# Gather-fed expert layer: the rest of the query projection in eighths of a block per slot, more early gather buffers, second tile's routing from slot 95

## The chip, the cores and the metric

One NeuronCore of a Trainium2 chip runs the whole program. Its engines run side by side, each through its own list of instructions, and meet at semaphores: PE (matrix products), DVE (vector operations), ACT (activations, copies), POOL (here small vector work and the indirect DMAs) and SP (plain DMAs). The metric is the device time of one execution in microseconds.

## What is computed

A transformer block of 512 tokens with 1024 channels and an expert layer, then a second block. The change is within the expert layer:

```python
def peer_ffn(h, wq, keys, u_tab, v_tab):
    ...
        q = (xb @ wq).reshape(T, PEER_HEADS, 2, PEER_KHALF)
        s = jnp.einsum('thpc,hpnc->thpn', q, keys)
        v1, i1 = lax.top_k(s[:, :, 0], PEER_TOPK)
        v2, i2 = lax.top_k(s[:, :, 1], PEER_TOPK)
        ...
        idx = jnp.take_along_axis(cidx, pos, axis=-1)
        gate = jax.nn.softmax(sc, axis=-1)
        ug = jnp.take(u_tab, idx, axis=0)
        act = jax.nn.gelu(jnp.einsum('td,thkd->thk', xb, ug), approximate=False)
        vg = jnp.take(v_tab, idx, axis=0)
        return jnp.einsum('thk,thkd->td', gate * act, vg)
```

Each token picks 8 x 16 = 128 of 16384 experts. Its 128 rows of u and v (8 KB for a pair) are gathered from HBM.

## The kernel before

`experts` (from L1935) works on four token tiles of 128 tokens. A *slot* is one of the 128 picks of every token in the tile: POOL issues an indirect DMA that brings 128 rows of u and v, 1.05 MB, into a buffer (L2115 for tile 0, L2132 behind it); DVE takes the dot of each u row with its token (`dot_slot` L2636); ACT makes gelu, the weight and a diagonal matrix of it (`gelu_slot` L2370, three instructions, the last L2378); PE multiplies the diagonal by the v rows into an accumulator (`sum_slot` L2213, instruction L2218, four matmuls of fp32). Only then is the buffer free (`used`), for which POOL waits before it issues the gather that goes there. All engines go through the slots in order; the order of all else is written out by slot numbers.

Ahead of this stand the query projection (16 blocks of 128 columns: `products`, 24 fp32r matmuls over 8 input chunks in three parts, L2155 to L2157; ACT casts the high part of the weights, `high` L2334, DVE subtracts the low part, `low` L2529, and takes the block out of PSUM, `evacuate` L2534), the scores against the keys for tile 0 (`first_score` L2161, `take_first` L2338), the normed activations h2 (`make_h2` L2537 on DVE), their turning into token rows (`turn_h` L2169 on PE, `take_h` L2342 on ACT), and routing (`route` L2544 on DVE): per group of heads eight pieces of top-k and softmax work. Two blocks belong to a head.

Tile 0 starts while the projection is unfinished. Blocks 0 to 5 (`JOINED_FROM = 6`) come first. Block 6 to 15 go into slots 0 to 39 (`CHUNKS = 4`): PE does a quarter of a block (six matmuls), then the sum of the slot `LAG = 2` behind. As the late gather buffers share memory with the projection's weights, slots 0 to 39 go round `EARLY = 4` buffers (`uv_spare`, `uv_second`, the second half of `cands`, the second half of h2, the last of which waits until h2 is turned). From slot 40, when all products are done, there are eight. Routing of tile 0: head 0 ahead of all, then head 1 from slot 0, pairs of heads from slots 12, 28, 44, one piece after each dot (`FIRST_AT`). Tile 1: two halves of four heads, one piece after every fourth dot from slot 56; its scores stand on PE behind the sum of slot 52, their copies on ACT behind slot 54. Tiles 1 to 3 run with eight buffers; tile 2's routing is spread over tile 1. Between tile 0's last sum and tile 1's first stand on PE a closing reset product, `score(2)` and an opening one, and on ACT `store(0)` and `take_scores(2)`. In tiles 2 and 3 the FFN's first half is woven in, by slot too.

Of the kernel before, what the change touches and what calls it, by code (L numbers as in the profile page):

```python
# [18 lines left out]
ALU = mybir.AluOpType  # L19
# [7 lines left out]
KD = D // P  # L27
# [1639 lines left out]
def mixer_out(nc, o, x, lnw, lnb, consts, saved_in, gate, bonus, sel, first):  # L1667


    with ExitStack() as ctx:  # L1670
# [139 lines left out]
        def _(dve):  # L1810
# [77 lines left out]
HEAD_GROUPS = (slice(0, 1), slice(1, 2), slice(2, 4), slice(4, 6), slice(6, 8))  # L1888
# [46 lines left out]
def experts(nc, w, x, weight, keys, consts, uv_tab, norm_after, ffn_in, ffn_out, ffn_weight, next_w, kept):  # L1935
# [13 lines left out]
    with ExitStack() as ctx:  # L1949
# [34 lines left out]
        with ExitStack() as first:  # L1984
# [8 lines left out]
        uv = [uv_late[:, 0], uv_late[:, 1], uv_late[:, 3], uv_late[:, 4], uv_spare[:, :, :], uv_late[:, 5], uv_late[:, 6], h2_rows]  # L1993
        uv_early = [uv_spare[:, :, :], uv_second[:, :, :], uv_third, h2_rows]
# [23 lines left out]
        squared, squared_p, added, summed, rooted, scaled, h2_made, h_turned, h_taken = map(signal, (  # L2018
            "wq_squared", "wq_squared_p", "wq_added", "wq_norm_summed", "wq_rooted", "wq_scaled", "h2_made", "h_turned", "h_taken"))
# [30 lines left out]
        def rows_of(t, at):  # L2050

            return uv_early[at % EARLY] if t == 0 and at < JOINED else uv[at % GROUPS]

# [85 lines left out]
        def _(pe):  # L2139
# [111 lines left out]

            for n in range(JOINED_FROM):
                products(n)
# [7 lines left out]
                if n == JOINED_FROM - 1:  # L2261
                    for k in range(KD // 2):
                        turn_h(k)
            for c in range(JOINED):
                n, q = JOINED_FROM + c // CHUNKS, c % CHUNKS
                products(n, q * KD // CHUNKS, (q + 1) * KD // CHUNKS)
# [1269 lines left out]
```

## Time and profile before

| | us |
|---|---|
| median of 3 runs | 2935.97 (2935.08 to 2940.54) |
| the profiled execution, its own time | 2942.34 |
| its span in the profile | 2940.5 |
| PE busy | 2652.8 (90%) |
| DVE busy | 1882.7 (64%) |
| ACT busy | 1231.4 (42%) |
| POOL busy | 755.6 (26%) |

Times in the rows are from the span's start. In an instruction's row the first number is its start, the second its length, in brackets stands how long the engine sat idle before it and who released it; several like instructions in a row are merged (x4). A window's row has for PE, weight loads, DVE, ACT and POOL the busy time and number of instructions, then PE's granted clock (1.00 is full speed), the mean share of time in which the 16 DMA engines are busy, and GB/s. A busy share of the whole span says little here: the expert layer's four tiles are one stretch of some 1400 us, and in each part of it another resource ends last.

### The profile page before, as it was taken

To read this page: it belongs to the slowest core of one execution; us is meant where nothing else is said; L and a number is where in the kernel's file an instruction comes from. 1 tells how busy PE (TensorE), PEld (TensorE's weight loads), DVE (VectorE), ACT (ScalarE), POOL (GpSimd) and SP (SyncE) were. 2 spreads that over 40 slices of the span, in tenths; PEclk is the share of its full clock that TensorE was granted. 3 is DMA by queue.
4 is the path that set the end of the run, shared out by engine and by line. 5 is a ranking of instruction groups with operands and counts; after the bars stand their busy time and mean duration, and the time that the engine had idled before them with its cause. 6 is when DMAs were issued, how large, how long until landed. Compare 5 with 4: busy or idle time off the path is not lost. (4 is left out here: it accounts for less than half of the span.)

```text
span 2940.5 us, 43930 instructions
## 1 busy us (share of the span) xinstructions
PE 2652.8 (90%) x16052; PEld 1806.7 (61%) x16052; DVE 1882.7 (64%) x3737; ACT 1231.4 (42%) x2723; POOL 755.6 (26%) x684
## 2 busy tenths in 40 slices
PE   8979999977787788899999999999899998999998
PEld 6669866533333333355555555799766676788876
DVE  6966667878867757976666665576666635554422
ACT  5622234434434444555555544443345355322221
POOL 0223212344454444444344344000100001100000
PEclk9989999999999999999999999999999999999998
DMA  4220127999999999999999999656411212223231
GB/s 158 68 70 22 43 91 287 330 382 422 421 412 415 421 414 421 414 408 419 419 419 419 420 419 419 240 185 179 139 58 58 65 51 72 89 95 96 80 132 49
DMA packets 128590, 714.84 MB, mean 243 GB/s; under 512 B 14232, under 2 KB 17176, under 8 KB 61720
## 3 DMA queue, kind: packets, MB, share of 16 engines
q0 software_dynamic: 73728, 536.90, 44.6%
q1 hardware_dynamic: 53528, 173.37, 17.6%
q8 instruction: 119, 1.95, 0.3%
q10 hardware_dynamic: 1152, 2.10, 0.2%
q14 instruction: 63, 0.52, 0.0%
HBM read 707.07 MB, written 7.86 MB: 243 GB/s over the span
## 5 line engine op out<-in xcount | busy, mean ns | idle before, releaser
L2218 PE MATMUL expert_total<-uv_rows,h 128*128 128x512 f32 x1032 | 492.5, 614 | 90.4 <-ACT h L2378 89.8
L2132 POOL DMA_INDIRECT uv_rows<-in_peer_uv,expert_ids x288 | 344.0, 1194 | 411.2 <-PE expert_total L2218 237.8
L2639 DVE CUSTOM_DVE_ANT_0 uv_rows<-uv_rows,h_tok 128x1024 f32<-128x1024 f32 x258 | 312.4, 1224 | 171.7 <-DMA uv_rows<-in_peer_uv,expert_ids 169.4
L2218 PEld LDWEIGHTS expert_total<-uv_rows,h 128*128 128x128 f32 x1032 | 188.5, 194 | 353.5 <-ACT h L2378 184.7
L2374 ACT ACTIVATE expert_acts<-expert_dots 128x1 f32<-128x1 f32 x384 | 77.6, 202 | 508.6 <-DVE expert_dots L2639 508.0
L2195 PE MATMUL expert_total<-uv_rows,h 128*128 128x512 f32 x384 | 186.9, 634 | 41.9 <-ACT h L2368 41.9
L2658 DVE TENSOR_TENSOR ffn_half_w_lo<-uv_rows,ffn_half_w_hi 128x1024 fp32r<-128x1024 f32 (+1 forms) x136 | 162.3, 1194 | 82.3 <-ACT ffn_half_w_hi L2398 78.9
L2398 ACT CAST ffn_half_w_hi<-uv_rows 128x1024 fp32r<-128x1024 f32 (+1 forms) x136 | 137.8, 1014 | 113.6 <-PE score_out L2249 63.3
L2195 PEld LDWEIGHTS expert_total<-uv_rows,h 128*128 128x128 f32 x384 | 75.2, 203 | 150.8 <-issue 120.3
L2247 PE MATMUL score_out<-ffn_half_x_hi,ffn_half_w_hi 128*128 128x256 f32 x528 | 167.8, 318 | 0.0
L2631 DVE CUSTOM_DVE_ANT_0 uv_rows<-uv_rows,h_tok 128x1024 f32<-128x1024 f32 x96 | 116.3, 1225 | 69.0 <-DMA uv_rows<-in_peer_uv,expert_ids 68.3
L2378 ACT ACTIVATE h<-const_sb,expert_weights 128x128 f32<-128x128 f32 x384 | 154.3, 402 | 12.5
L2249 PE MATMUL score_out<-ffn_half_x_hi,ffn_half_w_lo 128*128 128x256 f32 x528 | 149.8, 284 | 0.0
L2248 PE MATMUL score_out<-ffn_half_x_lo,ffn_half_w_hi 128*128 128x256 f32 x528 | 149.7, 284 | 0.0
L299 PE MATMUL ffn_in_out<-ffn_h_hi,ffn_in_w_hi 128*128 128x512 f32 x350 | 141.0, 403 | 2.5 <-DVE ffn_in_w_lo L388 2.5
L301 PE MATMUL ffn_in_out<-ffn_h_hi,ffn_in_w_lo 128*128 128x512 f32 x350 | 140.0, 400 | 0.0
L300 PE MATMUL ffn_in_out<-ffn_h_lo,ffn_in_w_hi 128*128 128x512 f32 x350 | 140.0, 400 | 0.0
L2978 PE MATMUL mix_out<-h_hi,mix_w_hi 128*128 128x512 f32 x303 | 128.5, 424 | 3.1 <-DVE mix_w_lo L3252 3.1
L379 DVE TENSOR_TENSOR ffn_in_w_lo<-ffn_in_w,ffn_in_w_hi 128x1024 fp32r<-128x1024 f32 x43 | 52.7, 1225 | 108.2 <-ACT ffn_in_w_hi L329 108.2
L2980 PE MATMUL mix_out<-h_hi,mix_w_lo 128*128 128x512 f32 x303 | 120.2, 397 | 0.0
L2979 PE MATMUL mix_out<-h_lo,mix_w_hi 128*128 128x512 f32 x303 | 120.0, 396 | 0.0
L2218 PE MATMUL expert_total<-h 128*128 128x512 f32 x212 | 104.3, 616 | 16.2 <-ACT h L2378 16.2
(578 smaller groups left out, 6447.6 us busy)
## 6 DMA issues: line engine op xcount, KB each, us to landing
uv_rows<-in_ffn_w_in SPq DMA_DIRECT2D x88, 512.0 KB, 6.1
ffn_in_w<-in_ffn_w_in SPq DMA_DIRECT2D x43, 512.0 KB, 3.5
mix_w<-in_w_in SPq DMA_DIRECT2D x39, 512.0 KB, 3.5
uv_rows<-in_ffn_w_out SPq DMA_DIRECT2D x32, 512.0 KB, 4.2
last_w<-in_ffn_w_out SPq DMA_DIRECT2D x7, 1408.0 KB, 6.2
w_in<-in_w_in SPq DMA_DIRECT2D x19, 512.0 KB, 3.5
wq_w<-in_peer_wq SPq DMA_DIRECT2D x15, 512.0 KB, 4.0
uv_rows<-in_ffn_w_out SPq DMA_DIRECT2D x16, 384.0 KB, 3.7
```

Of the source, the lines that this page charges most:

```text
L299: nc.tensor.matmul(out[:, b], high, hi[:, k], start=(k == 0), stop=False)
L300: nc.tensor.matmul(out[:, b], high, lo[:, k], start=False, stop=False)
L301: mm = nc.tensor.matmul(out[:, b], low, hi[:, k], start=False, stop=(k == kt - 1))
L2132: nc.gpsimd.indirect_dma_start(out=uv[first + j].rearrange("p a d -> p (a d)"), out_offset=None, in_=uv_tab, in_offset=bass.IndirectOffset ...
L2195: mm = nc.tensor.matmul(total[:, t % 2, half], diag[:, b], v[b][:, half * T:(half + 1) * T], start=False, stop=False)
L2218: mm = nc.tensor.matmul(total[:, t % 2, half], diag[:, b], rows_of(t, at)[:, 1, half * T:(half + 1) * T], start=False, stop=False)
L2247: nc.tensor.matmul(ffn_bank(n), high, x_high, start=(k == 0), stop=False)
L2248: nc.tensor.matmul(ffn_bank(n), high, x_low, start=False, stop=False)
L2249: mm = nc.tensor.matmul(ffn_bank(n), low, x_high, start=False, stop=(k == blocks - 1))
L2378: nc.scalar.activation(diag[:, b], consts("ident"), ACT.Copy, scale=scale_[:, col]).then_inc(diagonals, 1)
L2639: a.tensor_tensor_reduce(out=rows, in0=rows, in1=h_tok[:, t], scale=1.0, scalar=0.0, op0=ALU.mult, op1=ALU.add, accum_out=dot[:, b:b + 1]) ...
L2658: a.tensor_tensor(f_lo[:, j % PARTS, some], f_raw[PLACE[j]][:, some], f_hi[:, j % PARTS, some].bitcast(F32), ALU.subtract).then_inc(f_part ...
```

## The change

Blocks 6 to 15 are cut in eighths (three matmuls), one per slot, so that the projection ends at slot 79. The early buffers are given out by a table (`places`): four as before up to slot 79, with one in rows of `qT` that are not yet written up to slot 16 and one more up to slot 46. A gather waits for the slot that had its buffer last (`FREED_BY`): six slots back, then five, then four; slot 84 waits for slot 79. DVE waits for the last slot in those rows before it evacuates blocks 8 and 12. Heads of tile 0 are routed one by one, from slots 0, 8, 19, 35, 51, 67 and 83. Tile 1's pieces come after every second dot, from slot 95 to 125, its scores behind slots 91 and 93. h2 is made in two steps, x times the norm's weight on ACT behind the squares, times rstd on POOL ahead of its gathers. The turns of h2 stand on PE ahead of each half of block 5, and ACT takes them before it waits for that block. The clearing of `zero` comes ahead of block 5 on DVE.

```diff
-HEAD_GROUPS = (slice(0, 1), slice(1, 2), slice(2, 4), slice(4, 6), slice(6, 8))
+HEAD_GROUPS = tuple(slice(h, h + 1) for h in range(PH))
...
-JOINED_FROM, CHUNKS, EARLY = 6, 4, 4
-JOINED = CHUNKS * (N_QUERY - JOINED_FROM)
-LAG = 2
-GROUP_FROM = {1: 0, 2: 12, 3: 28, 4: 44}
-SECOND_FROM = 56
+JOINED_FROM, LAG = 6, 2
+CHUNKS = [(n, k, k + width) for n in range(JOINED_FROM, N_QUERY) for width in (1,) for k in range(0, KD, width)]
+JOINED = len(CHUNKS)
+BLOCK_END = {c: n for c, (n, _, end) in enumerate(CHUNKS) if end == KD}
+GROUP_FROM = {1: 0, 2: 8, 3: 19, 4: 35, 5: 51, 6: 67, 7: 83}
+SECOND_FROM = 95
...
-            **{SECOND_FROM + 4 * n: (1, n % PIECES, HEAD_HALVES[n // PIECES], len(HEAD_GROUPS) + n // PIECES) for n in range(2 * PIECES)}}
+            **{SECOND_FROM + 2 * n: (1, n % PIECES, HEAD_HALVES[n // PIECES], len(HEAD_GROUPS) + n // PIECES) for n in range(2 * PIECES)}}
...
+EARLY_UNTIL = {"spare": JOINED - 1, "second": JOINED - 1, "third": JOINED - 1, "h2": JOINED - 1, "query8": 16, "query12": 46}
+LATE_PLACES = ("late0", "late1", "late3", "late4", "spare", "late5", "late6", "h2")
...
+            free = [name for name, until in EARLY_UNTIL.items() if at <= until]
+            name = min(free, key=lambda name: last.get(name, -1))
...
             for k in range(0, KD, 2):
                 nc.gpsimd.tensor_tensor(sq[:, k], x[:, k], x[:, k], ALU.mult).then_inc(squared_p, 1)
+            hold(pool, scaled, 2, pace_p)
+            for k in range(KD):
+                hold(pool, h2_weighted, k + 1, pace_p)
+                nc.gpsimd.tensor_tensor(h2[:, k], h2[:, k], rstd[:, :], ALU.mult).then_inc(h2_made, 1)
...
-                    if at >= EARLY:
-                        hold(pool, used, GROUPS + at - (EARLY if at < JOINED else GROUPS) + 1, pace_p)
+                    if FREED_BY[at] is not None:
+                        hold(pool, used, GROUPS + FREED_BY[at] + 1, pace_p)
...
+            def at_slot(at):
+                if at == 0:
+                    first_score(JOINED_FROM - 1)
+                if at - 1 in BLOCK_END:
+                    first_score(BLOCK_END[at - 1])
+                if at == SECOND_FROM - 4:
+                    pe.wait_ge(copied0, N_QUERY)
+                    pe.wait_ge(h_taken, KD)
+                    score(1)
...
             for n in range(JOINED_FROM):
-                products(n)
+                if n < JOINED_FROM - 1:
+                    products(n)
+                else:
+                    for k in range(KD // 2):
+                        turn_h(k)
+                    products(n, 0, KD // 2)
+                    for k in range(KD // 2, KD):
+                        turn_h(k)
+                    products(n, KD // 2, KD)
...
             for k in range(1, KD, 2):
                 nc.scalar.activation(sq[:, k], x[:, k], ACT.Square).then_inc(squared, 1)
+            for k in range(KD):
+                nc.scalar.activation(h2[:, k], x[:, k], ACT.Copy, scale=weight[:, k:k + 1]).then_inc(h2_weighted, 1)
...
                 if n + SLOT < N_QUERY:
                     low(n + SLOT)
+                if n in (8, 12):
+                    dve.wait_ge(used, GROUPS + LAST_IN[f"query{n}"] + 1)
                 evacuate(n)
...
-            for k in range(KD // 2):
-                make_h2(k)
             take_block(4)
-            for k in range(KD // 2, KD):
-                make_h2(k)
+            a.memset(zero[:, :], 0.0).then_inc(zeroed, 1)
             take_block(5)
-            a.memset(zero[:, :], 0.0).then_inc(zeroed, 1)
             dve.wait_ge(h_taken, KD)
```

## Rows read from the trace of the kernel before

**Rows 1.** The page, part 2: GB/s moved in 40 slices of 73.5 us.

```profile
GB/s 158 68 70 22 43 91 287 330 382 422 421 412 415 421 414 421 414 408 419 419 419 419 420 419 419 240 185 179 139 58 58 65 51 72 89 95 96 80 132 49
```

**Rows 2.** Windows of 466 to 594 and 664 to 704 us: busy, clock, DMA.

```profile
466.00:594.00 128.00, 122.40 (x405) 74.18 (x404) 98.73 (x266) 53.12 (x144) 44.26 (x39) 1.00 0.91 335
664.00:704.00 40.00, 31.43 (x67) 12.28 (x66) 32.17 (x91) 17.23 (x52) 17.82 (x18) 0.96 1.01 422
```

**Rows 3.** Timeline of PE, one slot: start us, us, instruction.

```profile
475.63 1.88 PE L2218 MATMUL expert_total<-cands,h 128*128 128x512 f32 x4
476.95 0.80 PE L2155 MATMUL expert_total<-h_hi,wq_w_parts 128*128 128x512 f32 x1
477.58 0.40 PE L2156 MATMUL expert_total<-h_lo,wq_w_parts 128*128 128x512 f32 x1
...
478.74 1.88 PE L2218 MATMUL expert_total<-h 128*128 128x512 f32 x4
```

**Rows 4.** Timeline of POOL: gathers of slots 7, 39 and 40.

```profile
481.43 0.94 POOL L2115 DMA_INDIRECT h<-in_peer_uv,expert_ids  x1 [1.97 <-PE expert_total L2218]
...
589.00 1.23 POOL L2115 DMA_INDIRECT h<-in_peer_uv,expert_ids  x1 [2.17 <-PE expert_total L2218]
594.76 0.94 POOL L2115 DMA_INDIRECT uv_rows<-in_peer_uv,expert_ids  x1 [4.53 <-PE expert_total L2157]
```

**Rows 5.** Timelines of DVE and ACT: slot 2's dot, its laid-out weight.

```profile
470.74 1.23 DVE L2639 CUSTOM_DVE_ANT_0 cands<-cands,h_tok 128x1024 f32<-128x1024 f32 x1 [1.22 <-DMA cands<-in_peer_uv,expert_ids]
...
472.57 0.40 ACT L2378 ACTIVATE h<-const_sb,expert_weights 128x128 f32<-128x128 f32 x1
```

**Rows 6.** DMA issues in 470 to 600 us; last column median to landing.

```profile
cands<-in_peer_uv,expert_ids POOLq DMA_INDIRECT x9, 6.9
h<-in_peer_uv,expert_ids POOLq DMA_INDIRECT x9, 6.3
```

**Rows 7.** DVE: first dot; and the window of the first head's routing.

```profile
465.56 1.23 DVE L2639 CUSTOM_DVE_ANT_0 uv_spare<-uv_spare,h_tok 128x1024 f32<-128x1024 f32 x1 [2.79 <-ACT h_tok L2344]
...
442.40:453.70 11.30, 11.30 (x54) 9.41 (x53) 10.54 (x44) 3.92 (x6) 0.00 (x0) 1.00 0.31 93
```

**Rows 8.** Timeline of ACT: four squares, then block 2's cast.

```profile
423.51 2.19 ACT L2425 ACTIVATE cands<-x 128x512 f32<-128x512 f32 x4
429.67 1.06 ACT L2336 CAST wq_w_parts<-wq_w 128x1024 fp32r<-128x1024 f32 x1 [3.97 <-DMA wq_w<-in_peer_wq]
```

**Rows 9.** Timelines of POOL and DVE while both work on x.

```profile
415.98 5.11 POOL L2097 TENSOR_TENSOR cands<-x 128x512 f32<-128x512 f32 x4 [35.83 <-POOLq L1670]
416.39 2.62 DVE L2705 SCALAR_TENSOR_TENSOR h_lo<-x,vec_sb,h_hi 128x512 fp32r<-128x512 f32 x2 [0.61 <-ACT h_hi L2420]
...
424.22 1.40 DVE L2705 SCALAR_TENSOR_TENSOR h_lo<-x,vec_sb,h_hi 128x512 fp32r<-128x512 f32 x2
```

**Rows 10.** Timeline of DVE: dots of slots 40 and 41.

```profile
600.53 1.23 DVE L2639 CUSTOM_DVE_ANT_0 uv_rows<-uv_rows,h_tok 128x1024 f32<-128x1024 f32 x1 [3.48 <-DMA uv_rows<-in_peer_uv,expert_ids]
...
604.08 1.28 DVE L2639 CUSTOM_DVE_ANT_0 uv_rows<-uv_rows,h_tok 128x1024 f32<-128x1024 f32 x1 [2.32 <-DMA uv_rows<-in_peer_uv,expert_ids]
```

**Rows 11.** DVE: second tile's first piece; window of slots 56 to 119.

```profile
648.35 1.65 DVE L2565 MAX8 key_vals<-key_scores 128x8 f32<-128x128 f32 x8 [5.61 <-ACT key_scores L2349]
...
641.50:803.80 162.30, 129.22 (x292) 54.20 (x291) 130.40 (x355) 65.00 (x202) 75.80 (x69) 0.94 1.01 417
```

**Rows 12.** DVE, PE, POOL at the tile's end: slots 127, 128, 136.

```profile
821.67 1.23 DVE L2639 CUSTOM_DVE_ANT_0 h<-h,h_tok 128x1024 f32<-128x1024 f32 x1 [1.26 <-DMA h<-in_peer_uv,expert_ids]
834.48 7.13 PE L2195 MATMUL expert_total<-uv_rows,h 128*128 128x512 f32 x16 [1.53 <-ACT h L2368]
837.27 1.35 POOL L2132 DMA_INDIRECT uv_rows<-in_peer_uv,expert_ids  x1 [8.60 <-PE expert_total L2195]
844.37 1.22 DVE L2631 CUSTOM_DVE_ANT_0 uv_rows<-uv_rows,h_tok 128x1024 f32<-128x1024 f32 x1
```

**Rows 13.** Timeline of PE: two sums after an idle time.

```profile
802.66 5.31 PE L2218 MATMUL expert_total<-uv_rows,h 128*128 128x512 f32 x8 [4.90 <-ACT h L2378]
```

More of the change, by code:

```diff
@@ L1992, in experts @@
         h2_rows = h2[:, 4:8].rearrange("p (a k) t -> p a (k t)", a=2)
-        uv = [uv_late[:, 0], uv_late[:, 1], uv_late[:, 3], uv_late[:, 4], uv_spare[:, :, :], uv_late[:, 5], uv_late[:, 6], h2_rows]
-        uv_early = [uv_spare[:, :, :], uv_second[:, :, :], uv_third, h2_rows]
+        place = {"spare": uv_spare[:, :, :], "second": uv_second[:, :, :], "third": uv_third, "h2": h2_rows,
+                 **{f"query{n}": qT[:, n:n + 4].rearrange("p (a k) t -> p a (k t)", a=2) for n in (8, 12)},
+                 **{f"late{j}": uv_late[:, j] for j in (0, 1, 3, 4, 5, 6)}}
+        uv = [place[name] for name in LATE_PLACES]
         u, v = [rows[:, 0] for rows in uv], [rows[:, 1] for rows in uv]
@@ L2050, in rows_of @@
         def rows_of(t, at):
-            return uv_early[at % EARLY] if t == 0 and at < JOINED else uv[at % GROUPS]
+            return place[PLACE_OF[at]] if t == 0 else uv[at % GROUPS]
         def source(n):
@@ L2260, in _ @@
                     first_score(n - 1)
-                if n == JOINED_FROM - 1:
-                    for k in range(KD // 2):
[L2263 to L2266, printed above, removed]
+            for c, chunk in enumerate(CHUNKS):
+                products(*chunk)
                 if c == 0:
-                    for k in range(KD // 2, KD):
-                        turn_h(k)
                     pe.wait_ge(zeroed, 1)
                     add_zero(0, start=True, stop=False)
-                if q == CHUNKS - 1:
-                    first_score(n - 1)
                 if c >= LAG:
                     sum_slot(0, c - LAG)
+                    at_slot(c - LAG)
             for t in range(TT):
@@ L2287, in _ @@
                         sum_slot(0, at)
-                        if at == JOINED:
-                            first_score(N_QUERY - 1)
-                        if at == SECOND_FROM - 4:
-                            pe.wait_ge(copied0, N_QUERY)
-                            pe.wait_ge(h_taken, KD)
-                            score(1)
+                        at_slot(at)
                 elif t == 1:
@@ L2425, in _ @@
                 nc.scalar.activation(sq[:, k], x[:, k], ACT.Square).then_inc(squared, 1)
+            for k in range(KD):
+                nc.scalar.activation(h2[:, k], x[:, k], ACT.Copy, scale=weight[:, k:k + 1]).then_inc(h2_weighted, 1)
             act.sem_inc(used, GROUPS)
             for n in range(JOINED_FROM):
+                if n == JOINED_FROM - 1:
+                    for k in range(KD):
+                        take_h(k)
                 act.wait_ge(done, n + 1)
@@ L2439, in _ @@
                     exponentials(1, HEAD_GROUPS[0])
-            for k in range(KD):
-                take_h(k)
             for at in range(SLOTS):
                 gelu_slot(0, at)
-                n = JOINED_FROM + at // CHUNKS
-                if at % CHUNKS == 2 and n < N_QUERY:
+                if at + 1 in BLOCK_END:
+                    n = BLOCK_END[at + 1]
                     act.wait_ge(done, n + 1)
@@ L2535, in evacuate @@
                 a.tensor_tensor(qT[:, n], gemm_bank(n), rstd[:, :], ALU.mult).then_inc(free, 1)
-            def make_h2(k):
-                a.scalar_tensor_tensor(out=h2[:, k], in0=x[:, k], scalar=weight[:, k:k + 1], in1=rstd[:, :],
-                                       op0=ALU.mult, op1=ALU.mult).then_inc(h2_made, 1)
             def row(x, h):
```

31 lines of the change are left out of this document (21 added, 10 removed).

## The prediction

> **What bounds the kernel now.** I read the 40 slices of the page first: from slice 8 (about 515 us) the core moves 330 GB/s and more, and from slice 10 to slice 25 (about 1840 us) 408 to 422 [rows 1]. Up to there lie the gathers of the four token tiles, 512 slots of 128 rows of 8 KB, 1.05 MB each. The windows tell two stages apart [rows 2]: in 466 to 594 us, slots 0 to 39 with the rest of the projection, PE is busy 122.4 of 128 us, DMA share 0.91 at 335 GB/s; in 664 to 704 DMA share is 1.01 at 422 GB/s and PE has 31.4 of 40. So the first 40 slots are not DMA-bound, all later ones are, at 1.05 MB / 0.422 = 2.49 us a slot. What is won in the first stretch reaches the end, as nothing behind it has spare DMA time until 1840, and the FFN behind that only shifts.
>
> What sets the first stretch is seen in one slot of PE [rows 3]: sum at 475.63, chunk from 476.95, next sum at 478.74, so 3.11 us. The first product behind a sum takes 0.63, the others 0.23 each ((478.74 - 477.58) / 5); six are a quarter block. The actual cadence is longer: slot 7's gather leaves at 481.43 and slot 39's at 589.00, 3.36 a slot [rows 4]; the rest is scores of blocks and the bursts of two-head routing on DVE.
>
> **Part 1, an eighth block per slot.** Each chunk has three products fewer: 3.11 - 3 x 0.23 = 2.42 us of PE a slot, 2.45 with one first_score (0.22) in eight. The forty quarters become eighty eighths, the same PE work in all. PE is no longer the bound: DMA needs 2.49, plus a weight block of 512 KB in eight slots (1.25 us, 0.16 a slot) while they last, 2.65.
>
> **Part 2, the buffers.** A buffer's round trip from the rows: dot to weights laid out 2.23 (dot 470.74, last activation ends 472.97) [rows 5], sum 1.88 and 0.81 until POOL issues (478.74 + 1.88, then 481.43) [rows 3, 4], issue to landing 6.3 to 6.9 in the four-buffer stretch [rows 6], 5.8 when the queue is empty (594.76 to 600.53) [rows 4, 10]. With gaps: 5.0 + 6.3 = 11.3, and I add 0.3 for dots that find DVE in a routing piece or a block's evacuation: 11.6. Bounds are 10.8 (the empty queue) and 12.4 (four times 3.11, what it was with PE queueing). Six buffers give 1.9 a slot and five 2.3, both under the DMA's 2.65, which counts; I take 2.65 for slots 6 to 16 and 2.70 for 16 to 46 (little slack with five), up to 2.95 as the upper bound. Four buffers from slot 47 on give 11.6 / 4 = 2.90, bounds 2.70 and 3.11. This is the part where the change is slower than the late stretch of before (2.49), but faster than 3.11.
>
> **Part 3, the start.** h2 moves from DVE to ACT and POOL, and its turning goes ahead of and into block 5. On ACT eight weightings of 0.55 (four squares took 2.19) are 4.4 us where it sat idle 3.97 until the weights came [rows 8]: 0.4 to 1 late, then ACT waits for PE again; nothing on the path. POOL has been idle; eight products at 1.28 (5.11 for four) [rows 9] are 10.2 us, over by 450 or a little later, when PE reaches the turns at 451.8. Block 5 now ends some 5 us later (four turns and the evacuations ahead of each half), and DVE needs block 5 done before the dots; but the eight turns behind it are gone. So the first dot stays at about 465.6 [rows 7], bounds 1.5 earlier and 3 later. What is won is that POOL's wait for the turned h at slot 3 ends about 5 us earlier, with slots 4 and 5 right behind it without a wait: six gathers are on their way by 464, the seventh leaves at about 471, and slot 6 has its dot at about 478.
>
> On POOL and DVE the rows show a price: while POOL multiplied (415.98 to 421.1) two DVE operations with two SBUF operands took 2.62 us, against 1.40 later [rows 9]. In 439 to 450 DVE has two weight splits and a few small ones of this kind: 1 to 3 us on the first head's routing (10.5 busy of 11.3 [rows 7]) and so on gather 0. It is covered, as three gathers lie ready before the dots start; 1 of it would show if the cover were gone. The Trainium skill ("SBUF — State Buffer", section "SBUF: two separate sides") says that a DVE instruction with two SBUF inputs and a GpSimd one that reads SBUF hold the pair exclusively, the loser blocking for the whole instruction. By that rule POOL's eight products are also pushed by each 1.2 us split, so h2 is whole at about 452; the sum would be the same or 1 longer, and without the rule the same.
>
> **Part 4, routing.** Seven single heads in place of one single and three pairs: the same lists. Eight pieces of one head take 10.5 us at most in eight slots, with dots 1.15 each (in a run): 19.7, against 8 x 2.49 = 19.9: no lag. For a pair it is up to twice the 10.5, over the 19.9. The scores of the second tile, which came late so that DVE sat 5.6 us before its first piece [rows 11], lose that wait: PE's sum of slot 91 is no longer late. Worth 3 to 4 us.
>
> The price is at the end of the tile. The window from slot 56 to slot 119 has all sixteen pieces and 64 dots: DVE 130.4 busy [rows 11], less 64 x 1.19 = 54 us of pieces. They had 60 slots and now have 30, slots 95 to 125. DVE needs 32 x 1.15 + 54 = 90.8 us from dot 95 to dot 127, DMA 79.6. DVE becomes the bound, dot 127 comes 11 us late. Eight buffers could swallow most of that (a cycle of 19.9 against 10.8 of trip: 9 us), but right behind slot 127 stands a serial piece that uses the same slack: tile's closing sum, score(2), its copies, the next reset, then slot 128's sum. From dot 127 (821.67) to gather 136 (837.27) it took 15.6 [rows 12], which hid in before. Now gather 136 leaves 15.6 after a late dot 127. PE will also be slow there: behind an idle time of 4.9 us (such a gap as the last piece leaves) two sums took 5.31 [rows 13] in place of 2 x 1.72 (1.32 + 0.63 - 0.23 by [rows 3]), the slower of the clock's two levels; I add 2.3, bounds 0 and 3.
>
> **The sum**, against the profiled execution (2942.3, span 2940.5), as the time at which slot 136 is ready, 844.4 in before [rows 12]: 478 + 10 x 2.65 + 30 x 2.70 = 585.5 (slot 46); + 34 x 2.90 = 684.1; + 1 for the last chunk that gather 80 waits for = 685.1, where before had 600.5 + 1.1 + 39 x 2.49 = 698.7 and lost some 5 more around the second tile's late scores (part 4), about 704. To slot 95: + 15 x 2.49 + 1.1 (the restart gap of 3.55 against 2.49 [rows 10]) = 723.5. + 90.8 = 814.3 for dot 127. + 15.6 + 2.3 + 5.8 = 838.0. So 6.4 us less: 19 won in the 80 slots, most of it given back by DVE at the tile's end. 2942.3 - 6.4 = 2935.9; the median of the three runs is 6.4 below the profiled one, so 2929.6 for the median.
>
> **Rivals.**
> - *The four-buffer stretch runs no faster than PE's old 3.11.* For it: landing medians up to 6.9 [rows 6], no slack at four. Against: 12.4 held PE's queue, which goes. 34 x 0.21 = 7 us more: 2936.7, no change. Chance 0.22.
> - *Slower: the trip, not PE, made the old 3.36.* Then 34 slots at 3.36 with four buffers cost 15.6 more than taken, and no more in the five-buffer part (4/5 of 3.36 is 2.69): 2945. It decides from 3.09 us a slot on. For it: 3.36 was measured with four buffers. Against: PE idle only 5.6 of the 128 us. Chance 0.12.
> - *The tile's end costs nothing:* DVE's pieces overlap more than 1.15 + piece suggests, or the eight buffers swallow both. Then slot 136 is ready at 723.5 + 41 x 2.49 = 825.6: 2917.2. For it: DMA share stayed 1.01 through all sixteen pieces in before [rows 2, 11]. Against: the 91 us are busy time of one engine in order. Chance 0.14.
> - *The early start doesn't happen,* POOL's products or block 5 being later than I think, and the eighths do the rest: 3 us less won, 2932.6, still in the forecast's own range. Its chance is within the forecast's.
>
> **How the numbers follow.** Forecast (2922 to 2936, the point 2929.6) 0.52 with the fourth; the others 0.22, 0.12, 0.14. The range: lower end the third rival, 2917; upper end five-buffer cadence 2.95 (+7.5) with four at 3.11 (+7): 2944. This kernel's measurement can tell 0.2%, 5.9 us, so faster is below 2930.1. The forecast's case stands astride it, 0.32 of its 0.52 below, since the point is below and two of its terms (0.3 on the trip, 2.3 of slow PE) have more room to shrink than to grow; with the third rival's 0.14 and 0.02 of the first: 0.48. Slower (above 2941.8): 0.12 and 0.03 of the first rival, 0.15. Same: the rest, 0.37.
>
> **What would show it.** Dots of slots 6 to 46 at 2.65 to 2.7 and 47 to 79 at 2.9; POOL's gathers 3, 4, 5 at about 461 to 464; slot 80 ready near 685; no 5.6 us wait of DVE at the second tile's first piece; DVE over 95% busy from slot 95 to 127, dot 127 near 814, gather 136 about 18 us behind it with the DMA rate falling before it. Wrong if slot 80 is later than 691 (then no gain is left), or if DMA stays at 420 GB/s across the tile's end (then the gain is three times mine).

## The result and the profile after

| | before | after |
|---|---|---|
| median, us | 2937.7 (2935.1 to 2940.5, 5 runs) | 2947.9 (2941.8 to 2955.5, 5 runs) |
| ratio of the two | | 1.0035 [1.0021, 1.0049] |
| span of the profiled execution | 2940.5 | 2943.2 |

The change is slower by about 10 us. The forecast was 2929.6 with a range of 2917 to 2944, and its largest single chance (0.48) was for faster: the sign is wrong, and the time lies outside the range.

The expert stage of after begins earlier in its profiled execution. The marker is the reciprocal of the root mean square, which both programs do ahead of anything that the change could delay: 435.45 us in before, here in after:

```profile
429.48 3.35 DVE L2762 RECIPROCAL ffn_rstd<-ffn_rstd 128x512 f32<-128x512 f32 x1
```

That is 5.97 us, and it says nothing of the change: in the nine other kernels below, whose code up to there is the same or nearly so, the marker falls anywhere from 430.9 to 436.2. All slot times below are therefore put on before's scale by adding the difference of the two markers. A slot's time is the start of its dot on DVE.

| slot | before | after | recorded forecast | after less before |
|---|---|---|---|---|
| 6 | 484.5 | 481.5 | 478 | -3.0 |
| 44 | 611.5 | 587.4 | | -24.1 |
| 46 | 617.5 | 592.3 | 585.5 | -25.1 |
| 80 | 704.0 | 701.4 | 685.1 | -2.6 |
| 95 | 741.6 | 739.3 | 723.5 | -2.2 |
| 127 | 821.7 | 833.1 | 814.3 | +11.4 |
| 136 | 844.4 | 856.3 | 838.0 | +12.0 |
| 144 | 866.7 | 880.3 | | +13.6 |
| 511 | 1866.2 | 1879.8 | | +13.7 |

The table already tells the story. A gain of 25 us stands at slot 46 and is gone by slot 80. Another 13.6 us are lost between slots 95 and 127, and from slot 144 to slot 511 nothing comes back, since those slots run at the DMA's pace in both kernels. The last dot is 13.7 us late on this scale, the median of the times only 10.2. What stands behind the last dot took 1069.3 us in after's profiled execution and 1074.4 in before's; over all eleven kernels it took 1069.3 to 1077.5, so this difference is within what single executions vary by.

Windows of after (us, then busy time and instructions of PE, PEld, DVE, ACT and POOL, granted clock, DMA share, GB/s): slots 6 to 46, slots 48 to 80, slots 95 to 127, and from dot 127 to slot 136.

```profile
475.60:586.40 110.80, 101.97 (x288) 52.80 (x287) 85.59 (x228) 51.51 (x142) 45.53 (x41) 0.98 0.98 394
593.90:695.40 101.50, 83.19 (x228) 39.89 (x227) 60.50 (x152) 36.71 (x108) 36.03 (x35) 1.00 0.92 336
733.40:828.30 94.90, 67.96 (x134) 26.33 (x132) 92.57 (x293) 35.60 (x107) 39.48 (x36) 0.91 0.98 397
829.00:850.40 21.40, 19.87 (x68) 10.57 (x67) 10.29 (x25) 9.72 (x30) 6.35 (x6) 0.95 0.59 212
```

In the first window DMA share is 0.98 at 394 GB/s, where before had 0.91 at 335 [rows 2]. In the second it falls to 336 GB/s although PE has 83.2 busy of 101.5 us and DVE 60.5: no engine is full and DMA isn't either. In the third DVE is busy 92.6 of 94.9. In the fourth DMA share is 0.59.

Two timelines of after. First the dots on DVE at both ends of the stretches (start us, us, instruction, idle time before and its releaser), slots 79, 80, 95, 127 and 136:

```profile
692.08 1.23 DVE L2676 CUSTOM_DVE_ANT_0 uv_spare<-uv_spare,h_tok 128x1024 f32<-128x1024 f32 x1 [1.83 <-DMA uv_spare<-in_peer_uv,expert_ids]
695.41 1.23 DVE L2676 CUSTOM_DVE_ANT_0 uv_rows<-uv_rows,h_tok 128x1024 f32<-128x1024 f32 x1 [1.49 <-DMA uv_rows<-in_peer_uv,expert_ids]
...
733.36 1.23 DVE L2676 CUSTOM_DVE_ANT_0 h<-h,h_tok 128x1024 f32<-128x1024 f32 x1 [1.24 <-DMA h<-in_peer_uv,expert_ids]
...
827.11 1.22 DVE L2676 CUSTOM_DVE_ANT_0 h<-h,h_tok 128x1024 f32<-128x1024 f32 x1
...
850.36 1.22 DVE L2668 CUSTOM_DVE_ANT_0 uv_rows<-uv_rows,h_tok 128x1024 f32<-128x1024 f32 x1 [5.46 <-DMA uv_rows<-in_peer_uv,expert_ids]
```

POOL's gathers: slots 3 to 7, five in the four-buffer stretch, and 135 and 136 around the tile's end:

```profile
455.68 0.94 POOL L2146 DMA_INDIRECT h<-in_peer_uv,expert_ids  x1 [0.30 <-issue]
456.92 0.94 POOL L2146 DMA_INDIRECT qT<-in_peer_uv,expert_ids  x1 [0.30 <-issue]
458.16 1.77 POOL L2146 DMA_INDIRECT qT<-in_peer_uv,expert_ids  x1 [0.30 <-issue]
464.71 0.94 POOL L2146 DMA_INDIRECT uv_spare<-in_peer_uv,expert_ids  x1 [4.77 <-PE expert_total L2249]
467.34 1.93 POOL L2146 DMA_INDIRECT uv_second<-in_peer_uv,expert_ids  x1 [1.69 <-PE expert_total L2249]
...
595.79 0.94 POOL L2146 DMA_INDIRECT uv_spare<-in_peer_uv,expert_ids  x1 [2.95 <-PE expert_total L2249]
598.94 0.94 POOL L2146 DMA_INDIRECT uv_second<-in_peer_uv,expert_ids  x1 [2.21 <-PE expert_total L2249]
601.58 0.94 POOL L2146 DMA_INDIRECT cands<-in_peer_uv,expert_ids  x1 [1.70 <-PE expert_total L2249]
604.98 0.94 POOL L2146 DMA_INDIRECT h<-in_peer_uv,expert_ids  x1 [2.46 <-PE expert_total L2249]
608.80 0.94 POOL L2146 DMA_INDIRECT uv_spare<-in_peer_uv,expert_ids  x1 [2.89 <-PE expert_total L2249]
...
834.22 1.80 POOL L2163 DMA_INDIRECT h<-in_peer_uv,expert_ids  x1 [0.49 <-issue]
844.74 0.94 POOL L2163 DMA_INDIRECT uv_rows<-in_peer_uv,expert_ids  x1 [8.72 <-PE expert_total L2226]
```

### The profile page after: what moved, and what is told of

The parts are those of the page before. It is cut to its first block and busy times, and to the rows that moved or that the text cites. A ratio compares the mean times of both kernels' runs of the same rounds, so it can differ in the third digit from the quotient of the medians.

```text
span 2943.2 us, 44026 instructions
## 1 busy us (share of the span) xinstructions
PE 2653.7 (90%) x16052; PEld 1798.0 (61%) x16052; DVE 1889.3 (64%) x3780; ACT 1244.3 (42%) x2740; POOL 766.6 (26%) x692
## 5 line engine op out<-in xcount | busy, mean ns | idle before, releaser
L2249 PE MATMUL expert_total<-uv_rows,h 128*128 128x512 f32 x912 | 440.9, 619 | 70.7 <-ACT h L2415 70.3
L2676 DVE CUSTOM_DVE_ANT_0 uv_rows<-uv_rows,h_tok 128x1024 f32<-128x1024 f32 x228 | 276.9, 1225 | 153.1 <-DMA uv_rows<-in_peer_uv,expert_ids 150.9
L2249 PEld LDWEIGHTS expert_total<-uv_rows,h 128*128 128x128 f32 x912 | 167.1, 195 | 301.5 <-ACT h L2415 152.9
L2226 PE MATMUL expert_total<-uv_rows,h 128*128 128x512 f32 x384 | 188.8, 640 | 43.1 <-ACT h L2405 43.0
L2226 PEld LDWEIGHTS expert_total<-uv_rows,h 128*128 128x128 f32 x384 | 75.7, 203 | 152.1 <-issue 124.9
L2668 DVE CUSTOM_DVE_ANT_0 uv_rows<-uv_rows,h_tok 128x1024 f32<-128x1024 f32 x96 | 116.1, 1225 | 74.3 <-DMA uv_rows<-in_peer_uv,expert_ids 73.7
L2249 PE MATMUL expert_total<-uv_spare,h 128*128 128x512 f32 x224 | 108.6, 607 | 21.1 <-ACT h L2415 20.8
```

The lines of the kernel that those rows point to most:

```text
L2226: mm = nc.tensor.matmul(total[:, t % 2, half], diag[:, b], v[b][:, half * T:(half + 1) * T], start=False, stop=False)
L2249: mm = nc.tensor.matmul(total[:, t % 2, half], diag[:, b], rows_of(t, at)[:, 1, half * T:(half + 1) * T], start=False, stop=False)
L2676: a.tensor_tensor_reduce(out=rows, in0=rows, in1=h_tok[:, t], scale=1.0, scalar=0.0, op0=ALU.mult, op1=ALU.add, accum_out=dot[:, b:b + 1]) ...
```

## The experiments

All are made from after and timed beside before on the same chip. Before's median was 2937.0 to 2937.9 in all of them. "Theory 1" and "theory 2" are as each expectation defines them. The *trip* is the time from a gather's issue to the issue of the next gather into the same buffer: the rows land, the dot, the weights laid out, the sum, the issue.

**The four-buffer stretch.** If buffers set the pace from slot 47 on, taking the fifth away at slot 23 must give the slower pace from there.

```diff
-EARLY_UNTIL = {..., "query8": 16, "query12": 46}
+EARLY_UNTIL = {..., "query8": 16, "query12": 22}
```

> The changed kernel, but its fifth early buffer is given up after slot 22 in place of slot 46, so that gathers wait four slots back from slot 27 on and not from slot 47. In the changed kernel slots 8 to 44 had their dots 2.72 us apart and slots 44 to 80 3.17 apart. Theory 1 (the buffer's round trip sets the four-buffer stretch): the dots of slots 27 to 46 go from 2.72 to about 3.17 apart too, slot 80 comes 8 to 9 us later than in the changed kernel, and the time is that much longer, about 2957. Theory 2 (something that belongs to slots 47 to 79, such as single-head routing with block evacuations or the clock, made them slow): slots 27 to 46 stay at about 2.72 and the time stays at that of the changed kernel, about 2948.

Measured: 2957.2 (2948.0 to 2960.5), ratio 1.0065 [1.0045, 1.0085]. Dots 27 to 44 took 51.5 us here, 47.4 in after, and 44.2 to 48.5 in the eight other kernels that have five buffers there. The windows of just these slots, this kernel's and then after's:

```profile
539.60:591.10 51.50, 45.49 (x126) 22.08 (x125) 32.59 (x80) 20.31 (x58) 17.26 (x18) 1.00 0.96 365
```

```profile
534.00:581.40 47.40, 43.79 (x124) 22.07 (x123) 32.46 (x79) 19.97 (x57) 22.76 (x18) 1.00 0.99 394
```

3.03 us a slot against 2.79, and PE's busy share falls from 0.92 to 0.88. Over slots 27 to 44 it loses 4.1 us, and by slot 48 it is 8 us behind after (3.2 of these stood at slot 27, which is no more than other kernels differ by there); at slot 80 it is 5.8 behind, where 8 to 9 were expected. The pace follows the number of buffers, with the same PE and DVE work: theory 1, with 3.03 a slot in place of the expected 3.17. This kernel is 9 us above after, 6.7 at the last dot.

**The routing of the second tile.** The second half of tile 1's routing (eight of its sixteen pieces) is left out, with semaphores kept; its picks are copies of the first half's.

```diff
+                if turn == len(HEAD_GROUPS) + 1:
+                    ...
+                        a.tensor_copy(idx[:, t, slots], idx[:, t, 0:SLOTS // 2])
+                    ...
+                    return
```

> The changed kernel with the second half of tile 1's routing left out: heads 4 to 7 of tile 1 take over the picks and gates of heads 0 to 3, and the eight pieces at slots 111 to 125 are one or more tiny DVE fills each, some 27 us of DVE work fewer. Theory 1 (DVE's routing pieces, one after every second dot, are the bound at the tile's end and their lateness adds to the serial step between the tiles): the 15.8 us that the changed kernel lost between slots 95 and 144 against the kernel before shrink to 1 to 4, the time falls by 12 to 15 us, to about 2934. Theory 2 (the loss there is of the transition itself: slow PE clock, score and copies): it stays within 3 us of the changed kernel, about 2946.

Measured: 2936.0 (2928.2 to 2944.9), ratio 0.9998 [0.9984, 1.0011]. Slots 95 to 127:

```profile
733.80:819.20 85.40, 68.74 (x140) 27.31 (x139) 67.38 (x198) 37.30 (x111) 43.84 (x36) 0.92 0.99 404
```

DVE has 67.4 of 85.4 us busy in place of 92.6 of 94.9, and dots 95 to 127 take 83.0 us in place of 93.75. From 95 to 144 this kernel loses 3.5 us on before where after loses 15.8. So DVE's work in this stretch is what made the second loss. The stretch didn't reach the DMA's 79.6, since the first half's eight pieces in 16 slots still hold DVE up: dots 95 to 111 took 47.4 us as in after, dots 111 to 127 35.6 in place of 46.4. Of what this kernel is ahead of after, 3.1 us stood already at slot 95, where both have the same code: that part is no effect of the change.

**Fewer four-buffer slots.** Blocks 12 to 15 in quarters as in before: the projection ends at slot 63, all eight buffers are there from slot 64.

```diff
-CHUNKS = [... for width in (1,) for k in range(0, KD, width)]
+CHUNKS = [... for width in (1 if n < 12 else 2,) for k in range(0, KD, width)]
```

> The changed kernel, but only blocks 6 to 11 in eighths (slots 0 to 47) and blocks 12 to 15 in quarters (slots 48 to 63), so that the eight buffers are there from slot 64 on; routing at the same slots. Theory 1 (the trip with four buffers gives 3.17 a slot, and a quarter's 3.10 of PE fits under it): slots 48 to 63 keep 3.2 to 3.3 a slot, slots 64 to 79 go at 2.49, 16 x 0.68 = 11 us less at slot 80; the tile's end stays late, so about 2937 to 2940. Theory 2 (PE's load counts in that stretch beside the trip, as both queue up): slots 48 to 63 go at 3.5 or more, and the gain is 5 us or less, about 2943 or more.

Measured: 2942.8 (2938.4 to 2947.0), ratio 1.0015 [1.0006, 1.0025]. Slots 48 to 64, then 64 to 80:

```profile
602.40:653.90 51.50, 50.36 (x161) 28.98 (x159) 32.68 (x80) 19.87 (x57) 19.52 (x19) 1.00 0.91 334
653.90:694.50 40.60, 29.61 (x63) 10.87 (x64) 27.96 (x73) 17.32 (x52) 26.38 (x19) 1.00 1.01 420
```

With four buffers and quarter blocks a slot takes 51.5 / 16 = 3.22 us, PE busy 50.4 of 51.5; with four buffers and eighths it took 101.5 / 32 = 3.17. Halving PE's chunk hardly moved the pace: one bound stood right behind the other. As soon as the buffers are eight, the pace is 2.54. Slot 80 comes 7.6 us earlier than in after, where theory 1 had 11, and the tile's end stays as dear (+16.4 from slot 95 to 144 against before). The paces are theory 1's, the time is not: it lies between what the two theories said.

**Both, and the routing spread.** Quarters as above, heads 6 and 7 routed eight and sixteen slots sooner, and tile 1's pieces from slot 79 on in every third slot.

```diff
-GROUP_FROM = {1: 0, 2: 8, 3: 19, 4: 35, 5: 51, 6: 67, 7: 83}
-SECOND_FROM = 95
+GROUP_FROM = {1: 0, 2: 8, 3: 19, 4: 35, 5: 51, 6: 59, 7: 67}
+SECOND_FROM = 79
...
-            **{SECOND_FROM + 2 * n: ...
+            **{SECOND_FROM + 3 * n: ...
```

> As the one before (eighths to slot 47, quarters for slots 48 to 63), and besides it heads 6 and 7 of tile 0 are routed from slots 59 and 67 in place of 67 and 83, and tile 1's pieces come after every third dot from slot 79 on in place of every second from 95. By both parts of theory 1: 11 us less at slot 80 as there, and at three slots a piece DVE needs 3.45 + 3.4 of 7.47 us, so the loss at the tile's end is gone as well, 13 to 15 us: 2920 to 2925, 12 to 17 us under the kernel before (2938). If the tile's end was not DVE's: 2935 to 2938.

Measured: 2932.4 (2925.8 to 2938.2), ratio 0.9981 [0.9972, 0.9990]: faster than before, by 5 us where 12 to 17 were expected. Slot 144 lies 3.5 us ahead of before. The window from dot 127 on, and then PE's two sums at its start with their own window, and the dot of slot 125 on DVE, show a part that was not counted:

```profile
811.20:836.20 25.00, 23.47 (x72) 12.14 (x73) 12.48 (x27) 11.18 (x35) 6.50 (x7) 0.89 0.79 314
...
811.07 6.43 PE L2249 MATMUL expert_total<-uv_rows,h 128*128 128x512 f32 x8 [4.78 <-ACT h L2415]
...
811.07:817.30 6.23, 6.23 (x8) 2.70 (x9) 4.10 (x9) 1.80 (x6) 0.94 (x1) 0.56 1.01 421
...
808.79 1.22 DVE L2676 CUSTOM_DVE_ANT_0 uv_rows<-uv_rows,h_tok 128x1024 f32<-128x1024 f32 x1 [0.18 <-DVE expert_gate L2658]
```

Dots 95 to 127 now go at the DMA's pace (79.8 us), but the last piece stands behind dot 124: dot 125, whose rows had landed at 804.4, waits for it until 808.79, and PE sits idle for 4.8 us. Its next two sums run at a granted clock of 0.56 and take 6.43 us, where two sums take 3.60 at full clock in the next kernel. Gather 136 leaves 19.5 us behind dot 127, against 15.6 in before, and dot 127 to slot 136 takes 25.1 us, against 22.7.

**The same, three slots sooner.**

```diff
-SECOND_FROM = 79
+SECOND_FROM = 76
```

> The mixed version (eighths to slot 47, quarters to slot 63, tile 1's pieces every third slot), with the pieces from slot 76 in place of 79, so that the last comes at slot 121 in place of 124. There slots 128 to 144 took 47.4 us, against 42.5 in the kernel before and 39.8 of pure DMA. Theory 1 (a piece of 5.6 us four slots ahead of the serial step between the tiles leaves DVE late into it): 3 to 5 us of that come back, time about 2928, 8 to 10 us under the kernel before. Theory 2 (the step is longer for another reason, the sum of all lateness since slot 80): no difference, 2932.

Measured: 2928.0 (2923.2 to 2937.7), ratio 0.9971 [0.9961, 0.9982], the lowest median of all, 9.9 us under before and 20 under after. Its interval overlaps that of the kernel above: the times make it likely that the three slots help, and don't show it. Its slots 64 to 127, and from dot 128 to slot 136:

```profile
650.90:813.50 162.60, 128.52 (x282) 53.53 (x283) 142.62 (x414) 70.74 (x209) 79.51 (x69) 0.92 1.01 420
814.00:835.10 21.10, 19.57 (x70) 10.52 (x69) 10.92 (x24) 9.48 (x29) 8.45 (x8) 1.00 0.84 335
```

420 GB/s over 162.6 us with both the late heads and all of tile 1's routing in it: DVE 142.6 busy, which is 0.88 and leaves room for the dots. A DMA share of 0.84 is left at the tile's end. PE's clock is 1.00 there, gather 136 leaves 17.6 us behind dot 127, and slots 128 to 144 took 45.3 us against 47.4 in the kernel above: 2.1 us came back, where theory 1 had 3 to 5. That is its direction, and the late last piece is one cause; the rest, 45.3 against before's 42.5, stays open.

**The start.** The old way to make h2: on DVE behind block 4, all turns behind block 5.

```diff
-            for k in range(KD):
-                hold(pool, h2_weighted, k + 1, pace_p)
-                nc.gpsimd.tensor_tensor(h2[:, k], h2[:, k], rstd[:, :], ALU.mult).then_inc(h2_made, 1)
...
+            for k in range(KD // 2):
+                make_h2(k)
```

> The changed kernel with the old start: h2 made by DVE around block 4, its turns on PE behind block 5 and behind the first eighth of block 6, ACT taking them behind the casts, none of it on POOL. So POOL's gather of slot 3, and 4 and 5 behind it, leave some 10 us later than in the changed kernel. Theory 1 (DMA bounds slots 6 to 46, so that what the start wins stays until the end): slot 8 comes 3 to 5 us later and slot 80 by as much, time about 2952. Theory 2 (the four-buffer stretch, not tied to DMA, takes the difference up, or the block 5 order costs what the early gathers win): within 1.5 us of the changed kernel's 2948.

Measured: 2949.6 (2946.6 to 2959.8), ratio 1.0040 [1.0024, 1.0055], which the intervals don't tell from after's. Its gathers of slots 3 to 6:

```profile
461.82 1.88 POOL L2142 DMA_INDIRECT h<-in_peer_uv,expert_ids  x1 [5.29 <-PE score_out L2203]
464.00 1.36 POOL L2142 DMA_INDIRECT qT<-in_peer_uv,expert_ids  x1 [0.30 <-issue]
465.67 0.94 POOL L2142 DMA_INDIRECT qT<-in_peer_uv,expert_ids  x1 [0.30 <-issue]
466.91 1.15 POOL L2142 DMA_INDIRECT uv_spare<-in_peer_uv,expert_ids  x1 [0.31 <-issue]
```

From its own marker (432.22) gather 3 leaves at 29.6, in after at 26.2; but slot 6 has its dot at 45.5, in after at 46.1, and slot 8 at 54.1 and 54.0. The gathers that after sends 3.4 us sooner only queue: they land one behind the other. So theory 1's 3 to 5 us at slot 8 are out. This kernel's last dot is 3.8 us behind after's, which has grown only after slot 16 (0.1 there) and is no more than kernels with the same code differ by.

**A longer way from dot to sum.** Two kernels put copies of one column on ACT between the dot and the laid-out weights, in slots 47 to 79 alone. In the first, four copies:

```diff
+                for j in range(4 if t == 0 and 47 <= at < 80 else 0):
+                    nc.scalar.activation(sink[:, ...], dot[:, col], ACT.Copy)
```

> The changed kernel with a longer round trip in the four-buffer stretch alone: in slots 47 to 79 of tile 0 ACT does four more one-column copies into an unused tile before it lays out the weights, 0.7 to 0.9 us a slot, while it has 1.5 us or more idle in each. Theory 1 (a fixed round trip over four buffers sets the stretch, 12.7 us = 5.1 from dot to issue and 7.6 to landing): the pitch of dots 48 to 79 rises by a quarter of what is added, from 3.17 to about 3.36, slot 80 comes 6 to 7 us later and the time is 2954. Theory 2 (the gathers' DMA time is the bound there, share 0.91 to 0.93 of all 16 engines, 2.9 us of engine time a gather): the added time is taken out of the wait for landing, the pitch stays within 0.05 and the time within 2 us of 2948.

Measured: 2950.4 (2944.5 to 2955.4), ratio 1.0040 [1.0024, 1.0055]. The copies ran into each other, so the step from dot to weights grew by only 0.42 us (2.33 to 2.75), the mean from issue to dot fell by 0.55, and a slot took 3.14 us in place of 3.17. Theory 1's 3.36 did not come, theory 2's pace did. But within what the stretch varies (its 32 slots took 97.2 to 101.5 us in the four kernels that have the same code there, after among them) that is no change. A quarter of 0.42 us is a tenth of a us a slot, 3 us in the stretch: as an experiment it was too small to tell. In the second, seven copies, each waiting for the one before:

```diff
+                for j in range(7 if t == 0 and 47 <= at < 80 else 0):
+                    nc.scalar.activation(sink[:, 0:1], dot[:, col], ACT.Copy).then_inc(padded, 1)
+                    act.wait_ge(padded, 7 * (at - 47) + j + 1)
```

> A larger dose: the changed kernel with seven one-column copies on ACT, each waiting for the one before, about 1.7 us added between the gelu and the laid-out weights in slots 47 to 79. The small dose added 0.42 us to dot-to-weights and the wait for landing fell by 0.55, so the pitch did not move. Theory 1 (a fixed trip over four buffers): 1.7 / 4 = 0.42 a slot, slot 80 13 to 14 us later than in the changed kernel, 2962. Theory 2 (the gathers' own time is the bound at this depth, and the wait for landing is what is left over, down to a floor of 5.8 to 6.2 us): only what exceeds 7.3 - 6.0 = 1.3 us shows, 0.1 a slot, 3 to 5 us, 2951 to 2953. Issue to dot at or below 6.3 us.

Measured: 2958.5 (2954.4 to 2965.0), ratio 1.0074 [1.0052, 1.0096]: between the two expectations. The DMA issues of its slots 48 to 79, the last column the median time from issue to landing, and then after's:

```profile
uv_spare<-in_peer_uv,expert_ids POOLq DMA_INDIRECT x7, 5.5
cands<-in_peer_uv,expert_ids POOLq DMA_INDIRECT x8, 5.7
h<-in_peer_uv,expert_ids POOLq DMA_INDIRECT x8, 5.7
```

```profile
uv_spare<-in_peer_uv,expert_ids POOLq DMA_INDIRECT x8, 7.3
cands<-in_peer_uv,expert_ids POOLq DMA_INDIRECT x7, 7.1
h<-in_peer_uv,expert_ids POOLq DMA_INDIRECT x7, 7.1
```

The step from dot to weights grew by 2.02 us (to 4.35). The gathers, now further apart, landed faster, 5.5 to 5.7 in place of 7.1 to 7.3, which is about the 5.8 of an empty queue [rows 4, 10]; none of these landed in under 5.4. So 1.3 of the 2.0 us was absorbed and the rest wasn't: the trip grew from 12.72 to 13.65, a slot from 3.17 to 3.33, and slot 80 comes 7 us later than in after. The trip is thus no fixed sum (theory 1 had 13 to 14 us), nor is it the gathers alone (theory 2 had 3 to 5): its steps count, and its landing gives way.

**Half the bytes.** In slots 47 to 79 each gather brings half its bytes (4 KB a row in place of 8, and of other rows); the rest of the buffer is what was there.

```diff
+                    half = 47 <= at < 80
...
-                        out=rows_of(0, at).rearrange("p a d -> p (a d)"), out_offset=None, in_=uv_tab,
+                        out=rows_of(0, at)[:, 0] if half else ..., in_=uv_tab.rearrange("n (a d) -> (n a) d", a=2) if half else uv_tab,
```

> The changed kernel, but the gathers of slots 47 to 79 of tile 0 bring half the bytes: rows of 4 KB in place of 8 KB into the u half of the buffer, other rows than the picked ones, and the v half keeps what it had. Number of gathers, buffers and waits are the same. Theory 1 (fixed trip): issue to landing falls by the 1.25 us of transfer, the trip from 12.7 to 11.5, pitch 2.87, slot 80 10 us earlier, 2938. Theory 2 (the gathers' bytes at this depth are the bound): the pitch falls to what PE needs, 2.42 to 2.55, slot 80 20 to 24 us earlier, about 2926.

Measured: 2938.3 (2934.2 to 2944.8), ratio 1.0003 [0.9994, 1.0013]. The window of its slots 48 to 80, and its DMA issues in the same slots:

```profile
597.60:685.10 87.50, 82.34 (x230) 40.97 (x228) 60.51 (x154) 36.96 (x108) 41.47 (x36) 1.00 0.68 208
```

```profile
h<-in_peer_uv,expert_ids POOLq DMA_INDIRECT x8, 5.0
uv_spare<-in_peer_uv,expert_ids POOLq DMA_INDIRECT x7, 5.0
cands<-in_peer_uv,expert_ids POOLq DMA_INDIRECT x7, 4.9
```

The transfers are now far from filling DMA, 208 GB/s at a share of 0.68. From issue to dot it takes 5.26 us in place of 7.34, while the two other steps are as they were (2.33 and 3.09); the trip is 10.77, and a quarter of it, 2.69, is what a slot takes (2.73 in the window). It is 32 x (3.17 - 2.73) = 14 us less in the stretch, 12.2 less at slot 80 and 10.4 at the last dot against after. The time is theory 1's (2938), but the pace is between theory 1's 2.87 and theory 2's 2.42 to 2.55: issue to dot fell by 2.1 us, where theory 1 had counted 1.25 for the bytes. PE's and DVE's work, buffers and waits were as before; only the gathers' bytes (and which rows they bring) differed, and the pace followed their landing. It isn't a clean measure of the trip with short transfers, since PE is busy 82.3 of 87.5 us here, 2.57 a slot, and so close behind.

## Why the prediction was wrong, step by step

**The failed step is the four-buffer stretch in part 2: its landing time.** The sum had 5.0 + 6.3 + 0.3 = 11.6 us a trip, 2.90 a slot, bounds 2.70 and 3.11. Measured over slots 47 to 79 of after, as means: dot to weights 2.33, weights to the gather four slots on 2.96 (of slots 47 to 75, whose buffers a gather of the stretch takes), issue to dot 7.34. The first two sum to 5.29, where 5.0 was forecast; issue to dot had 6.3 + 0.3 = 6.6. From a gather to the one four slots on POOL's issues show 12.72, and a slot takes 3.17. Slots 46 to 80 took 109.0 us in place of 99.6, and that 9.4 us is half of the miss. The 3.17 lies above even the upper bound, 3.11.

The 6.3 was a median [rows 6], and the other places had 6.9, 6.2 and 6.0. The mean landing over slots 4 to 39 of before was 6.42, so the median left out only 0.1. In slots 47 to 79 of after it was 7.17: the landing itself grew by 0.75 us as the gathers came closer, 3.12 us apart on average in place of 3.35. The other part, dots that find DVE busy, for which I had put 0.3, shrank from 0.88 to 0.18; tile 0's heads are routed one by one there, and not in pairs. So the mean from issue to dot stayed, 7.30 in before and 7.34 in after, and only the forecast had 6.6. The gathers are also bunched: in slots 47 to 79 of after, a few gathers follow at 2.4 to 2.9 us and then one or two at 3.4 to 4.4 (in the rows above 595.79, 598.94, 601.58, 604.98, 608.80), and behind close ones the time from issue to dot goes up to 8.7. That the bunches raised the mean isn't shown: in the longer-way kernel the intervals differ more (2.2 to 7.2 us) and the mean landing is 5.9. But the landing doesn't stay what it was when the rest of the trip is changed: that kernel shows it the other way round, landing down to 5.6 (median) when 2.0 us were added. Rival 1 (0.22) had nearly this pace, 3.11, and named the longer landing and the missing slack; its price of 7 us is near the 9.4. Rival 2 (0.12) said where the sum turns into a loss, 3.09 us a slot, and that line was crossed; its own price was put too high (3.36, which PE's queue did make in part: weights to the next gather took 3.70 in before and 2.96 in after). Neither gives the measured loss by itself: with this stretch as forecast, slot 136 would still have been 2.6 us later than in before, by the other terms below.

**Slot 6 at 478: 3.5 us too early.** The six early gathers left as forecast, 3 to 5 at 461.7 to 464.1 on before's scale, and the seventh at 470.7. But I took 6 to 7 us for its landing, as if the queue were short. The three gathers ahead of it had left within 2.5 us (455.68 to 458.16), one needs 2.5, and the seventh took 10.9 from issue (464.71) to dot (475.57), its landing behind theirs. Its dot, and the window up to there:

```profile
475.57 1.22 DVE L2676 CUSTOM_DVE_ANT_0 uv_spare<-uv_spare,h_tok 128x1024 f32<-128x1024 f32 x1 [1.02 <-DMA uv_spare<-in_peer_uv,expert_ids]
...
460.00:477.00 17.00, 15.83 (x48) 8.11 (x46) 13.47 (x43) 8.02 (x22) 5.68 (x5) 1.00 1.01 421
```

DMA share is 1.01 at 421 GB/s in 460 to 477 us. So the early start bought a queue, and the kernel with the old start shows it worth 0 us at slots 6 and 8, and not over 3 in the whole.

**Slots 6 to 46: right in kind, 3.3 us short.** 110.8 us for 40 slots, 2.77, where the sum had 107.5; the upper bound was 2.95. PE was no longer the bound, and 25 us stood gained. Part 1, the eighth of a block, did all that was costed.

**POOL's products beside DVE.** Eight took 12.25 us, 1.53 each, over at 445.4 (451.3 on before's scale, forecast 450 or a little later). DVE's split beside them:

```profile
433.10 12.25 POOL L2128 TENSOR_TENSOR h<-h,ffn_rstd 128x512 f32<-128x512 f32 x8 [18.27 <-DVE ffn_rstd L2762]
434.67 2.03 DVE L2572 TENSOR_TENSOR wq_w_parts<-wq_w,wq_w_parts 128x1024 fp32r<-128x1024 f32 x1 [0.53 <-ACT wq_w_parts L2373]
...
442.13 2.07 DVE L2572 TENSOR_TENSOR wq_w_parts<-wq_w,wq_w_parts 128x1024 fp32r<-128x1024 f32 x1
```

2.03 and 2.07 us against 1.23 for the same split at 428.33: the price that [rows 9] showed, and the rule of the Trainium skill ("SBUF — State Buffer", section "SBUF: two separate sides") fits it: each split lost 0.8, less than the one product of 1.28 that it may have had to wait out, and the eight products grew by 2.0 us in all, less than the two splits' 2.5. It was covered, as said: the first dot stood at 465.6 in both.

**Slots 80 to 95: right.** 38.0 us, forecast 38.4; no 5.61 us wait before tile 1's first piece [rows 11]. Before's own slot 80 was at 704.0, put at "about 704".

**The tile's end in part 4: right, 3 us small.** Dot 95 to 127 took 93.75 us, forecast 90.8; DVE 92.6 busy of 94.9, forecast over 95%. The sum behind the last piece ran at PE's slower level, a granted clock of 0.57 in 828.25 to 831.70:

```profile
828.25 3.45 PE L2249 MATMUL expert_total<-uv_rows,h 128*128 128x512 f32 x4 [4.33 <-ACT h L2415]
831.53 1.88 PE L2249 MATMUL expert_total<-h 128*128 128x512 f32 x4
```

3.45 for the sum after 4.33 us of idle time against 1.88 for the next, as two such sums had taken 5.31 in before [rows 13]. Dot 127 to gather 136 took 17.6 us (827.11 to 844.74), forecast 17.9, and it landed in 5.6, forecast 5.8. The kernel without the second half of the routing confirms DVE's part as the cause. Rival 3, that this end costs nothing, is out. Before hid its own serial piece in eight full buffers (slot 127 to 136 in 22.7 us, and DVE had its sixteen pieces done by slot 119 [rows 11]); here the late DVE and the serial piece use the same slack, and from slot 95 to 144 15.8 us are lost.

**The sum of misses.** Slot 6 3.5, slots 6 to 46 3.3, slots 46 to 80 9.4, slots 80 to 95 -0.4, DVE 2.95, tile's end -0.4: 18.3 us, which is 856.3 less 838.0 but for rounding. The median misses its forecast by the same 18.3 us (2947.9 less 2929.6); that both agree so closely is luck, as the profiled spans differ by 2.7 us only. The forecast of -6.4 at slot 136 became +12.0. "Wrong if slot 80 is later than 691 (then no gain is left)" is the line that came true: 701.4.

**The range** should have been wider at its upper end. The two uncertain paces were each given a bound from the rows of a PE-paced stretch, so the case of a mean of 7.3 from issue to dot had no place in it, though before's trace has just that mean: (5.3 + 7.3) / 4 = 3.15 a slot.

## What to carry to other kernels

When a bound engine is relieved in a loop with few buffers, take the trip from the mean time between issue and use, not from a median landing, and let the landing grow as the transfers come closer: here it went from 6.42 us at 3.35 us apart to 7.17 at 3.12. The pace came to 3.17 us a slot, where the trip by the old landing gave 2.90 and a transfer alone takes 2.49. What is added to or taken from one part of such a trip is partly made up by the landing. Work that is moved from an early stretch to a later one must be summed on its engine with what stands there, up to the next serial piece: here 54 us of routing in 30 slots cost more than was left of what the eighths had won, and spreading it over 45 slots with the quarters kept late turned +10 us into -10. The last piece should end some slots ahead of the serial piece: behind dot 124 it left PE idle for 4.8 us and its next two sums at the lower clock.

## What the runs showed of the hardware

An indirect gather of 128 rows of 8 KB took 5.5 to 5.7 us from issue to landing (median) in the longer-way kernel, whose gathers left 3.35 us apart on average, 5.8 to the dot in an empty queue, 7.1 to 7.3 in after's four-buffer stretch at 3.12 us apart, where 2.3 were under way on average (7.17 / 3.12), and 10.9 to the dot behind three that had left within 2.5 us; half the bytes took 4.9 to 5.0. The distance isn't all: in before, with quarter blocks of weights coming in beside, gathers also 3.35 us apart took 6.42 on average. The share of DMA time that one takes (an estimate, from the share, the window and the number of slots) is not fixed either: 0.92 x 101.5 us for 32 slots is 2.9 us a gather in after, and 0.86 x 107.9 / 32 = 2.9 in the kernel with the longer way, where backlogged ones take 2.49 at a share of 1.01. A share of 0.92 here is thus no sign that only 8% were left: the rate was 336 of 422 GB/s, 20% less.

What stays open is the shape of the bunches: why two or three close gathers are followed by a gap, and what it costs, wasn't tried apart. A fifth buffer in slots 47 to 79, the plainest test of the trip, wasn't tried either; taking the fifth away in slots 27 to 46 is the nearest to it.
